# Routing by one key per expert in two layers, the last layer's shared down-weights in the idle half of the residual, and another order of the queue's transfers

## The chip, the core and the metric

One Trainium2 chip, one of its cores. The kernel is one program with five instruction streams: TensorE (PE in the profile; PEld is its weight loading), VectorE (DVE), ScalarE (ACT), GpSimd (POOL) and SyncE (SP), which here issues all direct transfers. The metric is the device time of one execution in microseconds (us).

## The reference, cut to what matters

The model has two layers over 256 context tokens and 256 image tokens, 1024 features wide, all in fp32. Each layer is a mixer of three branches followed by a mixture of experts. The change lies in the experts' part and at its edges:

```python
def moe_ffn(xf, w_router, router_bias, w_e_gate, w_e_up, w_e_down, w_s_gate, w_s_up, w_s_down):
    scores = jax.nn.sigmoid((xf @ w_router).astype(jnp.float32))
    biased = scores + router_bias
    group_score = lax.top_k(biased.reshape(N, N_GROUPS, N_EXPERTS // N_GROUPS), 2)[0].sum(-1)
    _, gidx = lax.top_k(group_score, TOPK_GROUPS)                 # 4 of 8 groups
    ...
    _, eidx = lax.top_k(masked, TOP_K)                            # 8 of 64 experts
    wts = jnp.take_along_axis(scores, eidx, axis=1)
    wts = wts / (wts.sum(-1, keepdims=True) + 1e-20) * ROUTED_SCALE
    routed = routed_experts(xf, eidx, wts, w_e_gate, w_e_up, w_e_down)
    return routed + swiglu(xf, w_s_gate, w_s_up, w_s_down)        # a shared expert for all tokens
```

An expert is `(silu(x @ w_gate) * (x @ w_up)) @ w_down` with a hidden width of 256. Its gate and up weights are 2 MB and its down weights 1 MB, so one layer's 64 experts are some 200 MB. Layer 0 sends all 512 tokens through its experts, layer 1 (the last) only the 256 image tokens; nothing reads the context half of the residual once layer 1's mixer is past.

## The kernel before, in words

**Stages.** Each layer runs the mixer (`mla`, `ml`, `rw`), the merge of the branches (`mg_*`), a norm (`norm_*`), the routing (`ro_*`), and the experts: `px_*` in layer 0, `ex_*` in layer 1. Each stage has a function per engine, and each engine runs its own in program order. Semaphores order the engines: `pe.wait_ge(ro["sel"], ...)` lets PE wait until the selection is made. Every line with `ch.link(...)` waits for its own result, so DVE's chain in the routing is serial.

**Routing.** PE makes the router's product (L1429) and turns the tokens round (L1438) for a row-wise copy in HBM (`hidden_rows`, stored by SP at L1728 or L2152). DVE (`ro_dve`) selects 8 experts a token; `r_sel` is the 0/1 result (L1567). PE sums it into each token's position at its expert (L1445) and the expert's count (L1448, L1450). Two small products spread the expert ranks (L1454, L1456), and `place_rows` (L1496 on) turns each position into a row number `r_at`. The rows are cut in units of 128, each holding the tokens of one to four experts. Then, for each tile of 128 tokens and each of its 8 choices, 32 times in layer 0 and 16 in layer 1: DVE picks the k-th chosen row out of `r_at` (L1591), builds two one-hot blocks `r_hot` and `r_val` (L1601, L1603), and PE multiplies them (L1463) into the list of which token stands in which row. From it come the indices of the gathers (L1614, L1616; semaphore `ro["dk"]`).

**The shared expert.** PE computes its gate and up products in two halves (`shared_gate_up`, L1720), one between the rank product and the one-hot products, the other behind them. Its weights lie in the tile `branches` (`GU_W[3]`). ACT and DVE make the hidden values from them (`sh["sig"]`, `sh["hid"]`). In layer 1 the shared down product (L2281) runs ahead of the first unit, from the buffer `DN5[0]` in which expert 0's down weights stand afterwards.

**Experts.** For each unit PE turns the gathered rows (L1860; L2286 and L2301 in layer 1), multiplies them by the gate and up weights (L1870; L2296), turns the hidden values and multiplies by the down weights (L1885; L2310). Layer 0 stores each row in HBM and adds them up per token later (L1958, L2121). Layer 1 scales each row by its weight while copying it out of the bank (ACT L2418, DVE L2486) and adds it to its token at once (L2316). These row weights `SW` come by a long way: DVE makes the choice weights, SP stores them in HBM (L2180, `choice_weight_rows`), and POOL gathers one column for each unit (L2222).

**The weights' queue.** SP issues every weight load, in the order of `px_sync` and `ex_sync`. The slots are four (five in layer 1), and a load into a slot waits until PE has finished with what stood there. Layer 0's experts are ranked by load, so its first loads wait for the ranks (`ro["end"]`); in layer 1 experts 0 to 3 are fixed in their slots, so their loads wait only for the end of the merge.

## Time and profile before

| | us |
|---|---|
| median of 3 runs (2644.52 to 2645.91) | 2645.62 |
| the profiled execution | 2642.83 |
| its span | 2640.6 |
| layer 0: product of the one-hot blocks begins, ends | 863.7, 881.5 |
| layer 0: first unit's gate product begins | 905.24 |
| layer 1: first unit's gate product begins | 2123.20 |
| layer 1: last unit's last product ends | 2621.99 |

The profiled execution took 2.2 us more than the span of its instructions. The page has the busy time of each engine (PE 2402.9 us, 91%; DVE 785.4; ACT 570.4; POOL 146.3) and the same in 40 slices of 66 us. A digit is the busy share in tenths, PEclk is the granted clock of TensorE, and the DMA rows are the share of the 16 transfer engines and what they moved. A busy PE isn't PE at its peak.

### The profile page before, as it was taken

How to read it: one execution, taken by the hardware profiler on the slowest of the kernel's cores; microseconds unless marked ns; L12 is line 12 of the kernel's file. 1: busy time of each engine (PE TensorE's matmuls, PEld its weight loads, DVE VectorE, ACT ScalarE, POOL GpSimd, SP SyncE). 2: the span in 40 equal slices, each digit the busy share in tenths (PEclk: the TensorE clock that was granted, in tenths of full speed). 3: DMA queues.
4: the chain of work that ended last, by engine and by line, in shares of the span. 5: the costliest groups of instructions: out<-in, count | busy, mean ns of one | idle time of the engine just before them, and what ended most of it. 6: DMA issues, size and time to landing. Idle time of an engine off the chain costs nothing.

```text
span 2640.6 us, 41238 instructions
## 1 busy us (share of the span) xinstructions
PE 2402.9 (91%) x17286; PEld 1365.7 (52%) x17286; DVE 785.4 (30%) x1929; ACT 570.4 (22%) x1132; POOL 146.3 (6%) x154
## 2 busy tenths in 40 slices
PE   7999988999998898999998799988999799967997
PEld 3466477644445443333333556767788644433444
DVE  1364455311114431111111525555411521111112
ACT  3455223300002011111111144433210111100111
POOL 0000000000000111111111000000000011100100
PEclk9999999999997799999999899999999699988999
DMA  7101142411102699999999631122331599999993
GB/s 321 71 10 41 37 157 103 188 64 64 64 0 110 243 422 420 413 406 424 403 408 393 260 146 67 70 70 94 143 147 64 204 393 423 419 408 417 413 423 163
DMA packets 67640, 599.72 MB, mean 227 GB/s; under 512 B 13182, under 2 KB 13310, under 8 KB 25600
## 3 DMA queue, kind: packets, MB, share of 16 engines
q1 hardware_dynamic: 50032, 555.09, 51.9%
q0 software_dynamic: 17424, 41.99, 4.2%
q8 instruction: 137, 2.24, 0.3%
q14 instruction: 47, 0.39, 0.0%
HBM read 588.63 MB, written 26.75 MB: 233 GB/s over the span
## 4 chain that ended last, share of the span: by engine, by line
PE 82%; DMA 7%; DVE 5%; issue 3%; ACT 2%; another core or an unknown queue 0%; SPq 0%; ACTq 0%; DVEq 0%
PE bank L1870 10%; PE bank L1345 9%; PE bank L2296 7%; PE bank L292 6%; PE bank L1885 5%; PE bank L2310 3%; PE bank L1360 3%; PE bank L1350 3%; PE bank L2316 3%; PE bank L384 3%; DMA ring<-in_wexp 2%; DMA arena<-in_wexp 2%; PE bank L1034 2%; PE bank L1049 2%; PE bank L309 1%
## 5 line engine op out<-in xcount | busy, mean ns | idle before, releaser
L1870 PE MATMUL bank<-ring,arena 128*32 128x512 f32 (+2 forms) x1248 | 297.5, 610 | 16.5 <-issue 15.2
L1345 PE MATMUL bank<-normed,ring 128*128 128x512 f32 (+1 forms) x768 | 255.5, 486 | 0.0
L2296 PE MATMUL bank<-ring,arena 128*32 128x512 f32 (+2 forms) x832 | 193.4, 621 | 18.1 <-issue 16.6
L1345 PEld LDWEIGHTS bank<-normed,ring 128*128 128x128 f32 x768 | 145.9, 190 | 101.8 <-issue 91.8
L1870 PEld LDWEIGHTS bank<-ring,arena 128*32 128x32 f32 (+2 forms) x1248 | 94.7, 131 | 154.0 <-issue 152.0
L292 PE MATMUL bank<-normed,ring 128*128 128x512 f32 (+1 forms) x416 | 160.5, 544 | 0.0
L1870 PE MATMUL bank<-branches,arena 128*32 128x512 f32 (+2 forms) x400 | 134.3, 594 | 6.3 <-issue 6.3
L1885 PE MATMUL bank<-arena 128*32 128x512 f32 (+2 forms) x384 | 112.8, 596 | 7.0 <-DMA arena<-in_wexp 3.3
L292 PEld LDWEIGHTS bank<-normed,ring 128*128 128x128 f32 x416 | 78.4, 190 | 77.8 <-issue 75.3
L2060 DVE TENSOR_TENSOR arena<-bank,arena 128x256 f32<-128x256 f32 x43 | 18.3, 425 | 324.0 <-ACT arena L1979 324.0
L2296 PE MATMUL bank<-normed,arena 128*32 128x512 f32 (+1 forms) x256 | 92.9, 644 | 21.0 <-issue 18.1
L2296 PEld LDWEIGHTS bank<-ring,arena 128*32 128x32 f32 (+2 forms) x832 | 55.9, 123 | 102.4 <-issue 102.4
L1799 POOL DMA_INDIRECT arena<-hidden_rows,block_slots x42 | 42.7, 1016 | 1167.5 <-DVE block_slots L1616 883.9
L1885 PE MATMUL bank<-ring,arena 128*32 128x512 f32 (+2 forms) x440 | 102.0, 596 | 4.0 <-issue 2.0
L2480 DVE TENSOR_TENSOR arena<-bank,arena 128x256 f32<-128x256 f32 x27 | 11.5, 425 | 301.2 <-ACT arena L2412 301.2
L2316 PE MATMUL bank<-arena 128*128 128x256 f32 x432 | 97.7, 380 | 1.2 <-DVE arena L2486 1.2
L2310 PE MATMUL bank<-arena 128*32 128x512 f32 (+1 forms) x400 | 82.1, 630 | 17.4 <-issue 16.8
L2296 PE MATMUL bank<-branches,arena 128*32 128x512 f32 (+1 forms) x208 | 94.7, 609 | 0.0
L1350 PE MATMUL bank<-branches,ring 128*128 128x512 f32 (+1 forms) x256 | 90.4, 486 | 0.0
L2316 PEld LDWEIGHTS bank<-arena 128*128 128x128 f32 x432 | 80.0, 190 | 12.6 <-issue 2.8
L1360 PE MATMUL bank<-arena,ring 128*128 128x512 f32 (+1 forms) x256 | 83.1, 486 | 2.6 <-DVE arena L1389 2.6
L1372 ACT ACTIVATE arena<-bank 128x512 f32<-128x512 f32 (+1 forms) x48 | 23.4, 490 | 286.2 <-PE bank L1345 286.2
(484 smaller groups left out, 3828.5 us busy)
## 6 DMA issues: line engine op xcount, KB each, us to landing
ring<-in_wexp SPq DMA_DIRECT2D x87, 2048.0 KB, 14.5
ring<-in_wst SPq DMA_DIRECT2D x54, 2048.0 KB, 8.4
arena<-in_wexp SPq DMA_DIRECT2D x70, 1024.0 KB, 20.4
branches<-in_wexp SPq DMA_DIRECT2D x31, 2048.0 KB, 13.8
ring<-in_wexp SPq DMA_DIRECT2D x60, 1024.0 KB, 12.1
normed<-in_wexp SPq DMA_DIRECT2D x12, 2048.0 KB
arena<-expert_rows SPq DMA_DIRECT2D x6, 2048.0 KB, 11.0
branches<-expert_rows SPq DMA_DIRECT2D x2, 2048.0 KB, 14.4
```

The lines of the kernel that those rows point to most:

```text
L292: last = nc.tensor.matmul(bank[:, c0:], weights[:, k, j0:j0 + n], H[:, k, c0:], start=(k == 0), stop=(k == KD - 1))
L384: last = nc.tensor.matmul(ps[j][:, c0:], w[:, k, (j % 4) * P:(j % 4 + 1) * P], H[:, k, c0:], start=(k == 0), stop=(k == KD - 1))
L1034: last = nc.tensor.matmul(ps[4 + pr][h, cc], NL[pr][h, cc], XT[pr][h, cc] if v else ident[h, h], start=True, stop=True)
L1049: last = nc.tensor.matmul(ps[pr][h, cc], ZT[pr][h, cc], X[pr][h, cc], start=True, stop=True)
L1345: last = nc.tensor.matmul(ps[2 * (n % 4)][:, c0:], wg[:, k, i * P:(i + 1) * P], H[:, k, c0:], start=(k == 0), stop=(k == KD - 1))
L1350: last = nc.tensor.matmul(ps[2 * (n % 4) + 1][:, c0:], wb[:, k, :], BR[:, k, c0:], start=(k == b0), stop=(k == b1 - 1))
L1360: last = nc.tensor.matmul(ps[m % 4][:, c0:], w[:, k, (m % 4) * P:(m % 4 + 1) * P], YM[:, k, c0:], start=(k == 0), stop=(k == KD - 1))
L1870: last = nc.tensor.matmul(ps[2 + s][r0:r1, :], XT_[:, s, k * P + r0:k * P + r1], wt[:, k, :], start=(k == 0), stop=(k == KD - 1))
L1885: last = nc.tensor.matmul(ps[5 + h][r0:r1, :], HDT[:, s, k * P + r0:k * P + r1], wt[:, k, h * 512:(h + 1) * 512], start=(k == 0), stop=(k ...
L2296: last = nc.tensor.matmul(ps[5][r0:r1, :], XT_[:, s, k * P + r0:k * P + r1], w[:, k, :], start=(k == 0), stop=(k == KD - 1))
L2310: last = nc.tensor.matmul(ps[6 + h][r0:r1, :], HDT[:, s, k * P + r0:k * P + r1], w[:, k, h * 512:(h + 1) * 512], start=(k == 0), stop=(k = ...
L2316: last = nc.tensor.matmul(acc(m), YB[s][:, m * P:(m + 1) * P], OH[s], start=False, stop=False)
```

## The change

1. **Routing, both layers.** The running count over the selected experts (`r_cs`) goes, and its place is taken by `r_keyed = r_at * r_sel`: a row number where an expert is chosen and zero elsewhere. One `max` a tile gives the 8 largest, which replaces the 8 picks a tile. The one-hot blocks are built for a whole tile, two broadcast operations for 8 choices, in two buffers; ACT multiplies each choice's part of `r_val` by its number. The positions are read from the bank, and are computed in pieces between the rank products, the last one behind them.
2. **Shared gate and up.** They are cut in four. One quarter stands ahead of the wait for the selection, two behind the last positions, and one behind the one-hot products. Their weights are issued before the stores of `hidden_rows`.
3. **Layer 0.** PE waits for the shared hidden values behind the first unit's gate product instead of ahead of its rows; DVE makes the second half behind its first copy.
4. **Layer 1.** The shared down weights go to `R[:, :, 0:TC]`, the context half of the residual, and expert 0's down weights go straight to their slot. The load of the fifth expert waits for the first gathered rows and stands ahead of the fourth's down weights. The store of the choice weights stands behind the first two loads of the list.
5. **Between the layers** the next layer's small weights and first two chunks are issued before the wait for the residual.
6. **Norms.** A `Ln` over one column runs ahead of the wait for the sum.

```diff
         def norm_act_rs(act, ch, l, w, c0):
+            ch.link(nc.scalar.activation(arena(4640, 1), cn("eps", 1), ACT.Ln))
             act.wait_ge(norm["mm"], nth(w, l) * NORM["mm"] + 1)
...
+            shared_gate_up(pe, l, 0, 0)
             pe.wait_ge(ro["sel"], l * RO["sel"] + 1)
-            for t in range(t0, TT):
-                for u in range(t0, t + 1):
-                    nc.tensor.matmul(ps[2][:, t * E:(t + 1) * E], ...)
...
+            for t in range(t0, TT - 2):
+                positions(t)
             pe.wait_ge(ro["rk"], l * RO["rk"] + 1)
             nc.tensor.matmul(ps[1][:, E:2 * E], ...).then_inc(ro["ranked"], 1)
+            positions(TT - 2)
             pe.wait_ge(ro["rk"], l * RO["rk"] + 2)
             nc.tensor.matmul(ps[1][:, 2 * E:7 * E], ...).then_inc(ro["ranked"], 1)
-            shared_gate_up(pe, l, 0)
+            positions(TT - 1).then_inc(ro["pos"], 1)
+            shared_gate_up(pe, l, 0, 1)
+            shared_gate_up(pe, l, 1, 0)
...
+            for n, t in enumerate(range(t0, TT)):
+                act.wait_ge(ro["hot"], l * RO["hot"] + n + 1)
+                for k in range(HOT):
+                    part = r_val[:, n % 2, k, 0:PLAN[l].n]
+                    nc.scalar.activation(part, part, ACT.Copy, scale=cn("choice", 1, n * TOPK + k)).then_inc(ro["hc"], 1)
...
-            for i, (t, k) in enumerate(chosen):
-                ch.add(V.scalar_tensor_tensor(r_junk[:, i % 2, :], r_cs[:, t, :], float(k + 1), r_at[:, t, :], ALU.is_equal, ALU.mult,
-                                              accum_out=r_dk[:, t, k:k + 1]))
-                ch.settle()
+            ch.link(V.tensor_tensor(r_keyed[:, t0:, :], r_at[:, t0:, :], r_sel[:, t0:, :], ALU.mult))
+            for t in range(t0, TT):
+                ch.add(V.max(r_dk[:, t, :], r_keyed[:, t, :]))
...
+            for n, t in enumerate(range(t0, TT)):
+                if n >= 2:
+                    dve.wait_ge(ro["hotm"], l * RO["hotm"] + (n - 1) * HOT)
+                ch.link(V.tensor_tensor(r_hot[:, n % 2, :, :], bcast(cn("count", P), 1, HOT), bcast(r_p[:, t, :], 2, P), ALU.is_equal))
+                V.tensor_tensor(r_val[:, n % 2, :, 0:at.n], bcast(cn("count", at.n), 1, HOT), bcast(r_u[:, t, :], 2, at.n), ALU.is_equal).then_inc(ro["hot"], 1)
...
         def px_pe(pe, l, before):
-            pe.wait_ge(sh["hid"], l * SHN["hid"] + 4)
...
                 if u:
                     rows_down(u - 1)
+                else:
+                    pe.wait_ge(sh["hid"], l * SHN["hid"] + 4)
...
         def ex_sync(sp, before):
+            sp.dma_start(R[:, :, 0:TC], wexp[l, E, :, GU_N:].rearrange("p (k n) -> p k n", k=KD)).then_inc(shared_down_in[0], 16)
+            down(0, 0, dn5_in[0][0])
...
             gate_up(3, 3, gu5_in[3][0])
+            sp.wait_ge(*rows_arrived(0))
+            fifth = sp.value_load(EJI[0:1, 4:5], min_val=0, max_val=E)
+            gate_up(fifth, 4, gu5_in[4][0])
             sp.wait_ge(sh["hid"], l * SHN["hid"] + 4)
             down(3, 3, dn5_in[3][0])
-            sp.wait_ge(cb["c"], weights_made)
-            sp.dma_start(wrow..., WK[:, TT - NX:, :]).then_inc(weights_kept[0], 16)
+            first_later = min(i for i, (last_use, _, _) in enumerate(at.loads) if last_use)
+            for i, (last_use, kind, p) in enumerate(at.loads):
+                if i == first_later:
+                    sp.wait_ge(cb["c"], weights_made)
+                    sp.dma_start(wrow..., WK[:, TT - NX:, :]).then_inc(weights_kept[0], 16)
...
         def _(sp):
-                if l:
-                    sp.wait_ge(sh["res"], l * SHN["res"])
                 for n, (m, j) in enumerate(ORDER_OF_USE[l]):
+                    if l and n == 2:
+                        sp.wait_ge(sh["res"], l * SHN["res"])
```

How this stands on the engines. First PE in layer 0, from the turning of the tokens to the first unit; `normed,branches` is the shared gate and up product, `bank<-arena` with 76 columns is the product of the one-hot blocks. Before:

```order
L1438 MATMUL bank<-consts,normed 128x128 x32
L1445 MATMUL bank<-arena,consts 128x64 x10
L1448 MATMUL bank<-arena,consts 128x64 x4
L1450 MATMUL bank<-consts,arena 64x64 x4
L1454 MATMUL bank<-arena,consts 128x64
L1456 MATMUL bank<-arena,consts 128x320
L1720 MATMUL bank<-normed,branches 128x512 x16
L1463 MATMUL bank<-arena 128x76 x32
L1467 MATMUL bank<-arena,consts 128x64
L1720 MATMUL bank<-normed,branches 128x512 x16
```

PE in layer 0 at the same place, now:

```order
L1439 MATMUL bank<-consts,normed 128x128 x32
L1728 MATMUL bank<-normed,branches 128x512 x8
L1446 MATMUL bank<-arena,consts 128x64 x4
L1448 MATMUL bank<-consts,arena 64x64 x4
L1453 MATMUL bank<-arena,consts 128x64 x3
L1460 MATMUL bank<-arena,consts 128x64
L1453 MATMUL bank<-arena,consts 128x64 x3
L1463 MATMUL bank<-arena,consts 128x320
L1453 MATMUL bank<-arena,consts 128x64 x4
L1728 MATMUL bank<-normed,branches 128x512 x16
L1473 MATMUL bank<-arena 128x76 x32
L1728 MATMUL bank<-normed,branches 128x512 x8
```

Eight shared products have moved ahead of the counts, eight stay behind the one-hot products where sixteen stood, and the ten position products are spread over three places. (A product counts once here; the trace shows two instructions for each.)

Then SP in layer 1, around the store of the choice weights; `TENSOR_LOAD` and `ISA` are the reading of an expert's number and the waits of a load. Before:

```order
L2155 DMA normed<-in_wexp 128x4096
L2158 ISA
L2158 DMA arena<-in_wexp 128x2048
L2180 DMA choice_weight_rows<-choice_weights 128x2x8
L2183 TENSOR_LOAD block_experts
L2183 ISA x2
L2155 ISA
L2155 DMA ring<-in_wexp 128x4096
```

SP in layer 1 at the same place, now, from the fourth expert's down weights on:

```order
L2168 DMA arena<-in_wexp 128x2048
L2168 ISA
L2168 DMA arena<-in_wexp 128x2048
L2198 TENSOR_LOAD block_experts
L2198 ISA x2
L2165 ISA
L2165 DMA ring<-in_wexp 128x4096
L2198 TENSOR_LOAD block_experts
L2198 ISA x2
L2165 ISA
L2165 DMA ring<-in_wexp 128x4096
L2197 DMA choice_weight_rows<-choice_weights 128x2x8
```

Two loads of 2 MB, which wait for the first unit's gate product, now stand ahead of the store.

## Rows read from the trace of the kernel before

**Rows 1.** The page's slices of 66 us: share of the transfer engines, in tenths
```profile
DMA  7101142411102699999999631122331599999993
```
**Rows 2.** Windows: length, busy PE, PEld, DVE, ACT, POOL; clock, DMA share, GB/s
```profile
870.00:875.00 5.00, 5.00 (x20) 4.56 (x20) 4.67 (x19) 0.00 (x0) 0.00 (x0) 0.50 0.64 269
905.00:1460.00 555.00, 518.32 (x2894) 199.52 (x2894) 100.48 (x241) 83.22 (x171) 82.74 (x84) 0.98 0.98 403
2115.00:2603.00 488.00, 424.80 (x2610) 198.95 (x2608) 69.39 (x169) 53.94 (x105) 53.80 (x55) 0.94 0.99 411
```
**Rows 3.** Chain of waits through layer 0's routing: start, us, what
```profile
833.33 4.53 PE bank L1445 x20
...
840.65 0.22 DVE arena L1580
...
853.56 0.24 DVE arena L1591 x2
...
862.11 0.19 DVE arena L1594
...
865.89 15.59 PE bank L1463 x56
...
884.83 16.32 PE bank L1720 x32
...
905.24 7.76 PE bank L1870 x32
```
**Rows 4.** Timeline of both routings: start, us, engine, line, what, [idle before]
```profile
830.52 1.08 ACT L1481 ACTIVATE arena<-bank 128x512 f32<-128x512 f32 x2 [0.67 <-DMA hidden_rows<-arena]
831.31 0.61 DVE L1562 MAX8 arena<-arena 128x8 f32<-128x64 f32 x4
...
2067.40 1.08 ACT L1481 ACTIVATE arena<-bank 128x512 f32<-128x512 f32 x2 [0.19 <-PE bank L1438]
```
**Rows 5.** Operations like the new ones, lines by form: busy, mean ns
```profile
L1225 DVE TENSOR_TENSOR arena<-arena 128x1024 f32<-128x1024 f32 x1 | 1.2, 1218 | 0.0
L2032 ACT ACTIVATE arena<-consts,choice_weights 128x128 f32<-128x128 f32 x8 | 2.4, 390 | 0.0
```
**Rows 6.** Chain of waits, layer 1's routing and first units
```profile
2073.41 0.63 PE bank L1450 x4
...
2091.17 8.84 PE bank L1463 x32
...
2103.27 9.53 PE bank L1720 x32
...
2114.18 7.17 PE bank L2281 x32
2121.36 0.45 PE bank L2286 x4
...
2123.20 7.02 PE bank L2296 x32
...
2143.32 4.08 another core or an unknown queue
```
**Rows 7.** Timeline of SP (issue only) and POOL in layer 1
```profile
2112.82 0.33 SPq L2155 DMA_DIRECT2D branches<-in_wexp  x1
...
2129.90 0.38 SPq L2180 DMA_DIRECT2D choice_weight_rows<-choice_weights  x1
2131.04 9.60 SPq L2155 DMA_DIRECT2D ring<-in_wexp  x3
...
2136.03 1.00 POOL L2222 DMA_INDIRECT arena<-choice_weight_rows,block_slots  x1 [29.73 <-DMA choice_weight_rows<-choice_weights]
```
**Rows 8.** Chain of waits, later in layer 1: one load of 2 MB
```profile
2305.93 29.53 DMA ring<-in_wexp
```
**Rows 9.** Chain of waits between the layers, and at the last norm
```profile
1520.73 8.52 DMA ring<-in_wst
...
2626.51 1.28 ACT L267
```
**Rows 10.** Timeline of ACT between the layers
```profile
1526.97 7.97 ACT L286 ACTIVATE normed<-normed,modv,mod_scale 128x256 f32<-128x256 f32 x16 [0.76 <-DVE normed L273]
```

106 lines of the change are left out of this document (49 added, 57 removed).

## The prediction

> **What bounds the kernel.** I read the page first. Its slices [rows 1] show the transfer engines full in two stretches, 924 to 1452 us and 2112 to 2600 us. They are the two layers' experts, some 200 MB of weights each. The windows put numbers on it [rows 2]: in layer 0's expert stage the transfers are busy for 0.98 of the time, at 403 GB/s, and PE for 518 of 555 us; in layer 1's it is 0.99 and 411 GB/s, with PE busy for 425 of 488 us. So layer 0's stage is bound by both at once and layer 1's by the transfers. Neither gets shorter inside; what helps is that it starts earlier, or that the weights' stream has fewer holes at its start.
>
> The next view is the chain of waits through layer 0's routing [rows 3]. From the selection at 833 us to the first unit's product at 905.24 us, 72 us pass, in which transfers and PE do little for the experts. The chain alternates between DVE's serial steps, the product of the one-hot blocks, and the second half of the shared gate and up product. Layer 1's chain [rows 6] has the same steps, shorter, and two that layer 0 lacks: the shared down product (7.17 us) and, at 2143.32, a wait of 4.08 us of ACT for the gathered row weights.
>
> **Layer 0, step by step.**
> 1. A quarter of the shared product goes ahead of the counts. It can begin when ACT's last copy is done, 830.52 + 1.08 = 831.6 [rows 4]. It is 16 instructions. At full speed 32 of 256 columns take 7.17 us [rows 6], so 16 of 512 take 7.2; PE has idled before and starts at half clock, which I put at 1.4 us. It ends at 840.2. The counts took 840.65 - 837.86 = 2.8 us [rows 3] and take 1.4 to 2.8 now: DVE gets them 0.9 to 2.4 us later. I take 1.7.
> 2. The last position products, 8 instructions of 4.53 / 20 = 0.23 us [rows 3], stand behind the rank product, where DVE has 0.9 us of other work. Another 0.9 late; but a copy of 0.4 is gone. Together 2.2 us late.
> 3. The 32 picks take 862.11 - 853.56 = 8.55 us [rows 3]. In their place come one product over 256 elements (0.45) and four maxima, 0.61 [rows 4]. DVE gains 7.5 us here, and begins with the one-hot blocks at 857.7 instead of 863.0.
> 4. A tile's blocks are 1024 and 8 x 76 = 608 elements. The trace has no operation with such broadcast operands. The nearest row is 1024 elements without them, 1.22 us [rows 5]; so 1.2 + 0.8 = 2.0 us a tile. The bounds are that and twice as much. Two tiles are ready by 861.7.
> 5. PE isn't ready then. Behind the positions it has half of the shared product, which took 15.3 us there before and ends at 864.9 now. PE becomes what is late; this hides step 3 in part, and would hide step 4 up to 3.6 us a tile.
> 6. The one-hot product is 64 instructions. Before, it ran from 863.7 to 881.5 at the pace of DVE, and the granted clock fell to 0.50, which is 1.2 GHz [rows 2]. At PE's own pace an instruction takes 0.22 us at that clock (step 2) and 0.11 at 2.4 GHz, by the turning of rows, 0.45 for 4 [rows 6]. That bounds the phase at 8 and 14.5 us. I take 11.6, since it starts at full clock and such short products let it fall before. It ends at 876.5, 5.0 us earlier.
> 7. ACT multiplies 32 parts of 76 columns. Eight of 128 columns with a factor from memory take 2.4 us [rows 5], 0.3 each, less than PE's 0.22 x 2 for a choice. Hidden behind PE; if PE runs at full clock it costs up to 2 us.
> 8. Behind the one-hot product 16 instructions stand instead of 32: 7.2 us less of the 16.32 [rows 3]. Then the wait for the hidden values goes (they are needed 9 us later): of the 4.1 us from 901.15 to 905.24 some 1.4 remain, one turning and one copy. Together 9.9 us.
>
> Sum: 5.0 + 9.9 = 14.9 us earlier at the first unit, between 11 and 18 by the bounds. From there on nothing in layer 0's stage changes and transfers and PE are both full, so the whole stage moves by it.
>
> A rule of the Trainium skill speaks against step 7. ScalarE: Activation LUTs, What ACT_TABLE_LOAD costs, gives an activation 186 ns and 0.833 ns a column, 93 ns more for a factor from memory, and 93 less in a row of them. For 76 columns that is an estimate of 0.25 us each, 8.0 us in 32. By that rule the sum stays as long as PE needs more, and would lose some 2 us if it needed 0.22 a choice; the row of 0.3 us for 128 columns agrees with it.
>
> **Layer 1.** The same steps, in the same order. The quarter of the product runs from 2068.5 [rows 4] for 3.6 us, at a clock that the turning of the tokens before it keeps up, the counts are done 0.9 us earlier than 2074.04 [rows 6]. The picks give 3.6 us. PE is through with its 32 instructions of the shared product, 9.5 us long as those of L1720 [rows 6], at about 2089; the one-hot product takes 32 x 0.11 to 0.22 instead of 8.84 us and ends at 2094.6, 5.4 us earlier than 2100.0. Sixteen fewer instructions behind it give 3.6. The shared down product waits for the hidden values as before and takes its 7.17 us as before: the gathered rows are there before it is done, so it fills no wait. The first rows are turned 9.0 us earlier, at 2112.4, and the first gate product ends at 2121.2 instead of 2130.2.
>
> Here the queue's new order takes it back. The store of the choice weights was issued at 2129.90 and POOL went on at 2136.03 [rows 7]. Now it is issued behind two loads that wait for the first gate product: these go out at 2122.1 and 2123.2, and the store at 2123.7. Loads stand behind one another in this queue: one issued at 2305.93 landed 29.5 us later [rows 8], while 2 MB into an empty one took 8.5 [rows 9]. So the store waits for 4.2 MB, at 411 GB/s 10.2 us, and POOL goes on at 2135 to 2137, no earlier than before. ACT, ready at 2134.3, waits about 13 us instead of 4.1, and PE goes on at 2147.4 as before. What remains is the weights' stream: it starts 9.0 us earlier and has one load of 1 MB (2.5 us) less to do, but runs dry before the first two loads (3.7 us) and again while PE stands (5.3 us). That is 2.5 us, of which I take 1.5.
>
> DMA: Bandwidth & Descriptors, Queues, rings and completion order, of the Trainium skill states that each transfer engine takes its descriptors in the order of the ring and alternates between rings by packets. By this the store on SP's ring pays for both loads and the sum stands, while POOL's gathers, on a ring of their own, pay for a packet at a time.
>
> **The rest.** Between the layers the wait of 8.52 us for the first chunk goes [rows 9]. But PE's product there needs the normed tiles, which ACT makes one in 1.0 us from 1526.97 to 1534.94 [rows 10]; PE began at 1529.3 and ended one product behind ACT. It ends there again: nothing, at most 1 us. In the norms the table load stands ahead of the wait already. The new `Ln` over one column is hidden in four norms and stands behind the load of 1.28 us in the last [rows 9]: 0.2 us lost. The load in 1024 pieces of 1 KB into the residual has over 40 us; I cost it at nothing, and should it take three times as long, still nothing.
>
> **Sum.** 2642.83 - 14.9 - 1.5 + 0.2 = 2626.6 for the profiled execution. The median of the runs shown is 2.8 us above it, so 2629.
>
> **The rivals.**
> - *The store isn't late.* If it lands in some 6 us whatever stands before it, the row weights come by 2141 and the 9.0 us of layer 1 carry through, less the first hole, with the load saved: 8 instead of 1.5. 2623 us. For it: only 6.1 us [rows 7], behind several MB. Against it: the load of 29.5 us [rows 8].
> - *The blocks bind.* Broadcast operands at twice the time (4 us a tile), or ACT's parts in series with PE, lengthen the one-hot product to its old length. Only the fillers' gain of step 8 remains in layer 0: 9.9. 2634 us.
> - *The start is worth less.* Layer 0's stage keeps its end because the stream is what counts and its loads come no earlier. Then 1.5 and little more: 2642 us. Against it: the stream's first load behind the initial ones waits for the first gate product.
> - *Slower: the row weights.* PE in layer 1 stands until ACT has the first of them. Each further 2 MB ahead of the store or of POOL's gathers costs 5.1 us. From 2152 us on for POOL's first gather, 16 us later than before, layer 0's gain is eaten; with the gathers also late, 2650. Against it: just two loads stand ahead.
> - *The change doesn't do what it says*, PE's fillers standing on the path instead of in waits: 2644.
>
> **How the numbers follow.** Forecast 0.62, store not late 0.12, blocks bind 0.12, start worth less 0.07, slower 0.04, no effect 0.03. The forecast's own terms give 2625 to 2634; with the first two rivals the range is 2619 to 2637. Within 0.2%, which is 5.3 us, a measurement of this kernel can't tell a change from none. Faster 0.93, same 0.03, slower 0.04.
>
> **What would show it.** Right: the first gate product of layer 0 at about 890 and of layer 1 at about 2099 (2114 less 15); the one-hot product back to back on PE; ACT's wait for the row weights near 13 us; layer 0's expert stage unchanged at 555 us. Wrong: DVE or ACT ahead of every one-hot instruction in the waits; POOL's first gather of weights less than 14 us after the first gate product; an expert stage of layer 0 that has grown by what its start has won.

## The result, and the profile after

The changed kernel takes 2616.33 us (median of 4 runs, 2613.38 to 2616.77) against 2645.76 of the kernel before (now 4 runs, 2644.52 to 2652.57): a ratio of 0.9881, 95% interval 0.9863 to 0.9899. The forecast was 2629, range 2619 to 2637: the sign was right, but the time lies below the range, and the gain is 29 us where some 17 were forecast. The profiled executions differ by 26.55 us (2642.83 and 2616.28) where the sum had 16.2. Measured from landmarks that both kernels have (the norm's product, L262, the last thing ahead of the router; and the first gate product), this is where it arose:

| stretch (profiled executions, us) | before | after | forecast | measured |
|---|---|---|---|---|
| start to layer 0's norm product | 798.36 | 801.21 | 0 | +2.85 |
| from there to layer 0's first gate product | 106.88 | 87.55 | -14.9 | -19.33 |
| from there to layer 1's norm product | 1145.71 | 1145.55 | 0 | -0.16 |
| from there to layer 1's first gate product | 72.25 | 58.53 | -9.0 | -13.72 |
| from there to the end of the span | 517.40 | 521.26 | +7.7 | +3.86 |

The first line is unchanged code, at a mean granted clock of 0.98 in both profiles; over all profiles below it lies between 792 and 806. So differences of a few us are read from such stretches, not from spans.

The chain of waits of the changed kernel through layer 0's routing, to be held against [rows 3] (start, us, what):

```profile
834.67 8.65 PE bank L1728 x16
843.32 0.84 PE bank L1446 x8
844.16 0.62 PE bank L1448 x8
...
851.82 15.36 PE bank L1728 x32
867.18 1.76 PE bank L1473 x16
868.93 0.02 issue
868.96 1.24 DVE arena L1612
870.20 0.02 issue
870.22 0.80 DVE arena L1613
...
871.45 4.19 PE bank L1473 x32
...
878.72 8.77 PE bank L1728 x16
```

The picks (L1591) are gone from it; PE's own shared product (L1728) leads up to the one-hot product, which takes 8.5 us instead of 17.8. The windows over it, to be held against [rows 2] (length, busy PE, PEld, DVE, ACT, POOL; clock, DMA share, GB/s):

```profile
865.00:870.00 5.00, 5.00 (x34) 3.80 (x32) 1.04 (x1) 1.73 (x7) 0.00 (x0) 1.00 1.00 426
870.00:875.00 5.00, 4.25 (x36) 4.11 (x34) 2.90 (x4) 3.96 (x16) 0.00 (x0) 1.00 0.99 421
888.00:1445.00 557.00, 522.18 (x2899) 200.84 (x2898) 104.40 (x244) 85.33 (x177) 82.75 (x84) 0.98 0.98 404
2093.00:2576.00 483.00, 419.38 (x2574) 191.42 (x2572) 70.93 (x170) 53.22 (x104) 54.12 (x56) 0.93 0.98 406
```

The granted clock over the one-hot product is 1.00 (2.4 GHz) where it was 0.50. Layer 0's expert stage keeps its length and its rate (403 and 404 GB/s). Layer 1's is a little less full (406 GB/s instead of 411), and by the table above it lasts 3.9 us longer. In the page, the transfers' slices show the same two full stretches as [rows 1], each beginning earlier:

```profile
DMA  7101032511101899999999811122341699999993
```

Layer 1, the chain of waits, against [rows 6]:

```profile
2060.04 1.06 PE bank L1453 x4
...
2070.14 3.98 PE bank L1473 x32
...
2077.30 5.13 PE bank L1728 x16
...
2083.86 7.14 PE bank L2370 x32
2091.00 0.45 PE bank L2295 x4
...
2092.84 7.04 PE bank L2305 x32
...
2101.55 13.64 DMA choice_weight_rows<-choice_weights
2115.24 0.48 issue
2115.76 0.19 issue
2115.95 5.99 DMA arena<-choice_weight_rows,block_slots
2122.02 0.70 ACT arena L2437
```

The store of the choice weights does what the forecast said: issued behind two loads of 2 MB, it lets POOL go on after 14.4 us, and ACT waits 11.03 us for the row weights. PE stands for 8.5 us:

```profile
2115.00:2120.00 5.00, 0.00 (x0) 0.00 (x0) 0.00 (x0) 0.00 (x0) 3.14 (x4) 0.78 1.00 419
```

### The profile page after: what moved, and what is told of

Same layout as the page of the kernel before. It is cut to its first block, busy times and chain, and to the rows that moved or that the text cites. A ratio compares the mean times of both kernels' runs of the same rounds, so it can differ in the third digit from the quotient of the medians.

```text
span 2614.1 us, 41116 instructions
## 1 busy us (share of the span) xinstructions
PE 2390.2 (91%) x17286; PEld 1348.4 (52%) x17286; DVE 763.1 (29%) x1747; ACT 582.9 (22%) x1185; POOL 146.1 (6%) x154
## 4 chain that ended last, share of the span: by engine, by line
PE 82%; DMA 8%; DVE 4%; issue 3%; ACT 2%; SPq 0%; ACTq 0%; DVEq 0%; POOLq 0%
PE bank L1878 11%; PE bank L1346 9%; PE bank L2305 6%; PE bank L293 6%; PE bank L1893 5%; PE bank L2319 3%; PE bank L1361 3%; PE bank L1351 3%; DMA arena<-in_wexp 3%; PE bank L2325 3%; PE bank L385 3%; DMA ring<-in_wexp 2%; PE bank L1035 2%; PE bank L1050 2%; PE bank L310 1%
## 5 line engine op out<-in xcount | busy, mean ns | idle before, releaser
L1878 PE MATMUL bank<-ring,arena 128*32 128x512 f32 (+2 forms) x1248 | 298.3, 613 | 17.9 <-issue 16.2
L2305 PEld LDWEIGHTS bank<-ring,arena 128*32 128x32 f32 (+2 forms) x832 | 55.4, 124 | 102.9 <-issue 102.8
L1989 ACT ACTIVATE arena<-bank 128x256 f32<-128x256 f32 x43 | 16.5, 384 | 316.7 <-PE bank L1878 316.7
## 6 DMA issues: line engine op xcount, KB each, us to landing
ring<-in_wexp SPq DMA_DIRECT2D x87, 2048.0 KB, 14.4
ring<-in_wexp SPq DMA_DIRECT2D x59, 1024.0 KB, 10.3
branches<-expert_rows SPq DMA_DIRECT2D x2, 2048.0 KB, 13.8
```

Of the source, the lines that this page charges most:

```text
L1878: last = nc.tensor.matmul(ps[2 + s][r0:r1, :], XT_[:, s, k * P + r0:k * P + r1], wt[:, k, :], start=(k == 0), stop=(k == KD - 1))
L2305: last = nc.tensor.matmul(ps[5][r0:r1, :], XT_[:, s, k * P + r0:k * P + r1], w[:, k, :], start=(k == 0), stop=(k == KD - 1))
```

## The experiments

Sixteen kernels ran, two of them repeats; each is the changed kernel with one edit unless said otherwise. The table has all of them; in the text a single letter stands for the kernel whose name begins with it. Columns: the median; the ratio to the kernel before, timed beside it, with its interval; then, from the profile, us from layer 0's norm product to its first gate product (A), layer 0's expert stage from there to the shared down product (B), the same as A in layer 1 (C), and from layer 1's first gate product to the end of the span (D). The landmarks are read from PE's timeline, which puts them 0.1 us off the chain's.

| kernel | median | ratio | A | B | C | D |
|---|---|---|---|---|---|---|
| before | 2645.76 | 1 | 107.0 | 557.0 | 72.3 | 517.5 |
| changed | 2616.33 | 0.9881 (0.9863 to 0.9899) | 87.7 | 555.8 | 58.6 | 521.3 |
| s_changed_again | 2614.67 | 0.9883 (0.9865 to 0.9901) | 86.3 | 559.0 | 58.6 | 521.1 |
| f_picks_added | 2632.63 | 0.9954 (0.9935 to 0.9974) | 95.8 | 556.9 | 67.5 | 519.2 |
| n_picks_covered | 2619.55 | 0.9894 (0.9871 to 0.9917) | 89.1 | 556.7 | 60.5 | 519.4 |
| p_blocks_single | 2627.33 | 0.9925 (0.9903 to 0.9946) | 94.2 | 556.4 | 65.9 | 518.8 |
| q_picks_alone | 2636.58 | 0.9955 (0.9938 to 0.9973) | 102.1 | 556.8 | 68.8 | 518.6 |
| b_fillers_back | 2623.35 | 0.9916 (0.9888 to 0.9944) | 90.2 | 556.9 | 64.1 | 519.0 |
| c_hidden_wait | 2612.38 | 0.9882 (0.9852 to 0.9912) | 88.6 | 557.3 | 58.6 | 518.2 |
| a_store_first | 2618.04 | 0.9888 (0.9864 to 0.9912) | 86.3 | 556.0 | 61.4 | 519.1 |
| k_early_weights | 2610.85 | 0.9871 (0.9848 to 0.9895) | 86.3 | 556.5 | 58.4 | 518.2 |
| e_no_shared_down | 2611.22 | 0.9862 (0.9836 to 0.9888) | 87.8 | 556.1 | 53.3 | 523.6 |
| h_old_slot | 2615.10 | 0.9879 (0.9850 to 0.9908) | 87.9 | 556.0 | 58.5 | 521.3 |
| d_edges_back | 2616.04 | 0.9875 (0.9856 to 0.9894) | 87.9 | 559.8 | 58.5 | 521.4 |
| j_quarter_swap | 2612.40 | 0.9873 (0.9856 to 0.9890) | 81.9 | 560.1 | 55.4 | 521.4 |
| m_best | 2609.96 | 0.9855 (0.9838 to 0.9872) | 83.3 | 559.9 | 54.2 | 518.5 |
| m_again | 2606.43 | 0.9846 (0.9831 to 0.9862) | 81.8 | 559.9 | 54.5 | 518.3 |
| u_without_memsets | 2610.95 | 0.9861 (0.9843 to 0.9879) | 81.9 | 557.6 | 53.9 | 518.4 |

### Why the one-hot product became so short

```diff
+            for i in range((TT - t0) * TOPK):      # f_picks_added: behind the max of each tile
+                ch.add(V.scalar_tensor_tensor(r_junk[:, i % 2, :], r_keyed[:, t0, :], 1.0, r_at[:, t0, :], ALU.is_equal, ALU.mult, accum_out=...))
+                ch.settle()
+            shared_gate_up(pe, l, 1, 1)            # n_picks_covered: this too, ahead of the one-hot product
...
-            shared_gate_up(pe, l, 1, 1)            # and not behind it
```

> The changed kernel with 32 serial picks in layer 0 and 16 in layer 1 added ahead of the one-hot blocks on DVE (their results are not used), 8.5 and 4.3 us, so that DVE is as late there as before. PE then stands some 2 us in layer 0 and 5 us in layer 1 between its fillers and the one-hot product. Theory A (the product runs at PE's own pace and full clock, 0.13 us an instruction, whatever a pause of 2 us does): layer 0's first gate product comes 2 to 3 us later, layer 1's 4.3 later, 6 to 7 us in all. Theory B (the pause, or the pace of DVE, lets the clock fall to 1.2 GHz, as in the prediction's half): the one-hot product takes 12 to 15 us in layer 0, and the first gate product comes 7 to 10 us later, 11 to 15 us in all. If the picks were worth all their time, 12.8 us.

> The kernel with the added picks once more (32 and 16 serial operations of DVE whose results are not used), and in it PE's last quarter of the shared gate and up product moved ahead of the one-hot product, so that PE comes to it later than DVE and without a pause. Theory (PE's pause of 3.8 us ahead of the one-hot product let the clock fall; what DVE does meanwhile is nothing to it): the 64 instructions take 8 to 8.6 us in layer 0 instead of 12.8 with the pause, and the 32 in layer 1 take 4.0 instead of 7.1. Layer 0's first gate product: the picks are hidden, but the gathers start only behind them; 90 to 95 us from the start of the norm's product (87.7 in the changed kernel, 95.8 with the picks alone). Rival (the late picks themselves, or the pace of ACT's parts, slow the product): 12 us again in layer 0 and 7 in layer 1.

PE's timeline in layer 0, with the picks added (start, us, what, [idle before it and what ended that]):

```profile
848.17 16.23 PE L1732 MATMUL bank<-normed,branches 128*128 128x512 f32 x32
868.17 12.75 PE L1473 MATMUL bank<-arena 128*128 128x76 f32 x64 [3.76 <-ACT arena L1497]
```

and with the picks added and covered:

```profile
850.92 22.64 PE L1732 MATMUL bank<-normed,branches 128*128 128x512 f32 x48
873.39 3.69 PE L1474 MATMUL bank<-arena 128*128 128x76 f32 x32
877.83 4.17 PE L1474 MATMUL bank<-arena 128*128 128x76 f32 x32 [0.75 <-ACT arena L1497]
884.66 0.43 PE L1478 MATMUL bank<-arena,consts 64*128 64x64 f32 x2 [2.66 <-DVE arena L1633]
889.14 1.97 PE L1872 MATMUL bank<-consts,arena 128*128 128x128 f32 x8 [4.05 <-DMA arena<-hidden_rows,block_slots]
```

The windows over the one-hot product, first without cover, then with it:

```profile
870.00:875.00 5.00, 5.00 (x26) 5.00 (x25) 2.88 (x3) 3.95 (x16) 0.00 (x0) 0.50 0.73 308
875.00:880.00 5.00, 5.00 (x25) 5.00 (x25) 1.15 (x2) 2.58 (x9) 0.00 (x0) 0.50 0.01 3
```

```profile
875.00:880.00 5.00, 4.25 (x37) 4.11 (x36) 3.94 (x4) 2.58 (x11) 0.00 (x0) 1.00 1.03 437
```

Both kernels have the same picks and the same blocks. They differ in whether PE stands 3.76 us ahead of the product. With the pause the clock is at 0.50 in the product and its 64 instructions take 12.75 us; without it the clock stays at 1.00 and they take 8.6 from first to last. Theory B of the first run had the mechanism and the size in layer 0 (A of the table 8.1 to 9.5 us later, forecast 7 to 10), but not the sum: with C 8.9 us later it is 17 to 18 us, and 16 to 18 by the medians, where it said 11 to 15. The theory of the second held in layer 0's product; A is 89.1 where it said 90 to 95, and layer 1's product took 4.8 us instead of 4.0, behind a wait of 1.6 us that the cover left there. In layer 0 the covered kernel still waits 4.05 us for the gathered rows.

```diff
-                ch.link(V.tensor_tensor(r_hot[:, n % 2, :, :], ...))      # p_blocks_single
-                V.tensor_tensor(r_val[:, n % 2, :, 0:at.n], ...)
+                for k in range(TOPK):
+                    ch.link(V.tensor_scalar(r_hot[:, n % 2, k, :], cn("count", P), r_p[:, t, k:k + 1], None, ALU.is_equal))
+                    V.tensor_scalar(r_val[:, n % 2, k, 0:at.n], cn("count", at.n), r_u[:, t, k:k + 1], None, ALU.is_equal)
```

> The changed kernel with the one-hot blocks built one choice at a time, 16 operations a tile instead of two, all else (picks by max, ACT's multiplication, PE's order) as changed. Theory: a tile takes DVE 4.4 us as before instead of 2.0; two tiles are ready when PE comes from its fillers, the third and fourth are not; PE stands for them some 5 us in layer 0 and hardly in layer 1 (both tiles ready at about 2076 instead of 2070, so up to 5 us there too), and the clock falls in part of it. 5 to 9 us later in layer 0 and 4 to 7 in layer 1, 9 to 16 in all. Rival (PE's fillers cover it): less than 3 us in all.

A is 6.5 to 7.9 us later and C 7.3, 14 to 15 together; the median is 11 to 13 us above the changed kernel's. The theory held, with layer 1's part just above its range (4 to 7). PE waits 2.36 us for the third tile, and the product goes on at half clock:

```profile
866.36 4.05 PE L1473 MATMUL bank<-arena 128*128 128x76 f32 x32
872.76 3.70 PE L1473 MATMUL bank<-arena 128*128 128x76 f32 x16 [2.36 <-ACT arena L1497]
876.69 3.69 PE L1473 MATMUL bank<-arena 128*128 128x76 f32 x16 [0.23 <-ACT arena L1497]
```

```diff
-            for i, (t, k) in enumerate(chosen):                           # q_picks_alone, on the kernel before
-                ch.add(V.scalar_tensor_tensor(r_junk[:, i % 2, :], r_cs[:, t, :], float(k + 1), r_at[:, t, :], ...))
+            ch.link(V.tensor_tensor(r_cs[:, t0:, :], r_at[:, t0:, :], r_sel[:, t0:, :], ALU.mult))
+            for t in range(t0, TT):
+                ch.add(V.max(r_dk[:, t, :], r_cs[:, t, :]))
```

> The kernel before with one part of the change alone: the picks by one product and one max a tile (and the choice weights by the row number, in the same number of operations). DVE is 7.5 us earlier ahead of the blocks in layer 0 and 3.6 in layer 1, as the prediction had it. Theory (the parts need one another): PE's half of the shared product then ends behind DVE, and only PE's waits ahead of the one-hot product go, 2.4 us in layer 0 and 2.2 us in layer 1; the blocks are still built one by one, so the product keeps the pace of DVE. 4 to 5 us faster than before, about 2641. Rival (each part is worth its own time wherever it stands): 11 us, 2634.

In this kernel `r_dk` moves to a place that layer 1 clears before its choice weights are made, so their values in layer 1 are not the reference's; no instruction is more or less for it. The ratio is 0.9955, that is 7 to 16 us by its interval; A and C together are 8.4 us shorter. So the theory's 4 to 5 was too little, and the rival's 11 us lies in the interval. The waits ahead of the product go as expected, but the product gets shorter too (14.4 us instead of 17.8 in layer 0, 7.7 instead of 8.8 in layer 1), since it begins at full clock. The clock then falls, without a pause of PE, at the pace of the blocks:

```profile
863.00:868.00 5.00, 4.68 (x31) 3.72 (x29) 3.53 (x14) 0.60 (x1) 0.00 (x0) 1.00 1.00 424
868.00:873.00 5.00, 4.65 (x19) 3.81 (x18) 4.67 (x19) 0.00 (x0) 0.00 (x0) 0.65 0.98 418
873.00:878.00 5.00, 5.00 (x20) 4.55 (x19) 4.23 (x17) 0.00 (x0) 0.00 (x0) 0.50 0.38 161
```

The product's first instructions run back to back. From 866 us on two come in every 0.55 us, which is DVE's time for the blocks of a choice, with 0.11 us of idle between the pairs, and the clock falls in that stretch. PE's busy time (4.68, 4.65, 5.00 of 5.00 us) doesn't show it; the number of its instructions does.

### What the cut of the shared product is worth

```diff
-            shared_gate_up(pe, l, 0, 0)                 # b_fillers_back: not ahead of the counts
             pe.wait_ge(ro["sel"], l * RO["sel"] + 1)
...
+            shared_gate_up(pe, l, 0, 0)                 # behind the positions
             shared_gate_up(pe, l, 0, 1)
-            shared_gate_up(pe, l, 1, 0)
...
+            shared_gate_up(pe, l, 1, 0)                 # behind the one-hot product
             shared_gate_up(pe, l, 1, 1)
```

> The changed kernel with the shared gate and up product in two halves again: half of it behind the positions and half behind the one-hot product, none ahead of the counts. Theory: the 16 instructions behind the one-hot product come back on the path, 8.8 us in layer 0 and 5.1 us in layer 1; the counts come up to 5.6 us earlier in layer 0, which PE's fillers then hide from 0 to 5 us; so layer 0's first gate product is 4 to 9 us later and layer 1's 3 to 5 later, 7 to 14 us in all, most likely 10. Rival (the quarter ahead of the counts delays DVE's chain by as much as it saves): layer 0 less than 2 us later, the whole 3 to 5 us. Second rival (without the quarter the clock is low during the counts and at the start of the fillers): 2 us more than the theory.

A is 2.5 to 3.9 us later and C 5.5; the median is 7 to 9 us above, at the lower end of the theory's 7 to 14. In layer 0 the rival (less than 2 us) was nearer. PE's timeline shows why:

```profile
833.35 1.97 PE L1445 MATMUL bank<-arena,consts 128*128 128x64 f32 x8 [3.79 <-DVE arena L1583]
835.25 1.12 PE L1447 MATMUL bank<-consts,arena 128*64 128x64 f32 x8
...
843.49 14.92 PE L1728 MATMUL bank<-normed,branches 128*128 128x512 f32 x32
858.25 3.69 PE L1472 MATMUL bank<-arena 128*128 128x76 f32 x32
...
870.13 16.98 PE L1728 MATMUL bank<-normed,branches 128*128 128x512 f32 x32
```

Sixteen more instructions stand behind the product, and take 8.2 us more, but everything ahead of them is 5.6 us earlier against the norm's product (870.13 - 798.16 and 878.72 - 801.21 us, less the 0.1 between the two views). PE is busy from the counts on. The quarter can begin only when ACT's last copy is made, 33.6 us behind the norm's product, and the counts could begin at 35.2 without it: it fills 1.6 of the 3.8 us of wait. Behind it the counts run at full clock, 1.6 us instead of 3.0. The rest of the quarter is paid in either place.

```diff
+            pe.wait_ge(sh["hid"], l * SHN["hid"] + 4)   # c_hidden_wait: ahead of the first rows
...
-                else:
-                    pe.wait_ge(sh["hid"], l * SHN["hid"] + 4)
```

> The changed kernel with layer 0's wait for the shared hidden values ahead of the first rows again, and DVE making their second half ahead of its first copy. Theory: PE stands 2 to 3 us between its last quarter and the turning of the first rows, for ACT's sigmoid and two DVE products; layer 0's first gate product comes 2.7 us later (2.0 to 3.2), the rest of the kernel is the same: + 2.7 us. Rival (the gathered rows are late anyway): less than 0.5 us.

PE waits 2.14 us ahead of the first rows, where it had not waited; A is 0.9 to 2.3 us later, less than the theory's 2.7. The median can't show it (2612.4, below the changed kernel's).

### Layer 1's row weights

```diff
+            sp.wait_ge(cb["c"], weights_made)           # a_store_first: ahead of the list
+            sp.dma_start(wrow..., WK[:, TT - NX:, :]).then_inc(weights_kept[0], 16)
             for last_use, kind, p in at.loads:
...
+            for part in range(3):                       # k_early_weights: this too
+                choice_weights(ch, l, part)
             rows_in(0)
-            for part in range(3):
-                choice_weights(ch, l, part)
```

> Layer 1's store of the choice weights stands ahead of the list of loads again; nothing else differs from the changed kernel. Theory (the store pays for the two loads ahead of it): POOL's first gather of row weights comes some 6 us behind the store instead of 14.4 us, so at about 2106 to 2108 instead of 2115.95; ACT's wait of 11.0 us before its first scaled copy shrinks to 1 to 5 us, and PE resumes 5 to 8 us earlier. At the end 4 to 6 us are left, about 2611. Rival (the weights' stream sets layer 1's end, as the prediction had it): PE resumes earlier, but the end moves by less than 1.5 us, 2615 to 2616. Second rival (the store pays for what is in flight anyway): POOL's gather comes no earlier and nothing moves.

> As the kernel with the store first, and DVE makes layer 1's choice weights ahead of its first copy of gathered rows, in the 8.85 us in which it waits for PE, instead of behind it. Theory: the choice weights (6.5 us of DVE) are ready at about 2091 instead of 2100, the store lands by 2097, the row weights are there by 2104, and ACT never waits for them; PE's pause between unit 1's hidden values and its down product is about 7 us or less (12.8 in the changed kernel). Against the changed kernel 6 to 8 us earlier at that point and 5 to 8 at the end, about 2610. Rival (the stream sets the end): less than 1.5 us, 2615 to 2616. Second rival: DVE's copy of rows comes late, up to 0.5 us lost at the first gate product.

SP's, POOL's and ACT's timelines, with the store first:

```profile
2100.14 0.38 SPq L2194 DMA_DIRECT2D choice_weight_rows<-choice_weights  x1
```

```profile
2102.45 1.00 POOL L2235 DMA_INDIRECT arena<-choice_weight_rows,block_slots  x1 [23.92 <-DMA choice_weight_rows<-choice_weights]
```

```profile
2111.89 0.69 ACT L2435 ACTIVATE arena<-bank,arena 128x512 f32<-128x512 f32 x1 [1.28 <-PE bank L2317]
```

and SP's and POOL's with the weights made early:

```profile
2088.77 0.38 SPq L2194 DMA_DIRECT2D choice_weight_rows<-choice_weights  x1
```

```profile
2099.60 1.00 POOL L2235 DMA_INDIRECT arena<-choice_weight_rows,block_slots  x1 [21.45 <-DMA choice_weight_rows<-choice_weights]
```

ACT's wait of 11 us is gone in both. From layer 1's first gate product to ACT's first scaled copy it is 29.2 us in the changed kernel and 19.5 in these two, as in the kernel before (2142.63 - 2123.20 = 19.4). At the end it is worth much less. The stretch D is 521.1 to 521.4 in the changed kernel and those that differ from it little, 518.2 to 519.1 here; but some kernels with the late store (b, c, p, f, n) have 518.2 to 519.4 too. The medians are 2618.0 and 2610.9 against 2616.3 and 2614.7.

So the first theory, 4 to 6 us at the end, failed: alone the early store shows nothing there. Its profile has a part of the reason in code that the edit doesn't touch: the shared products of layer 1 took 9.7 and 6.6 us instead of 8.3 and 5.2, and C is 61.4. With the weights made early the median is 4 to 5 us lower (theory 5 to 8, rival under 1.5), which the intervals don't separate from nothing. The closest pair is j and u below, which differ in these two edits alone and were timed side by side: D is 521.4 and 518.4, the medians are 2612.4 and 2611.0. Of 9.7 us some 3 arrive in the stretch D; what of it reaches the whole is not shown.

```diff
-                for m in range(KD):                     # e_no_shared_down
-                    for k in range(2):
-                        nc.tensor.matmul(acc(m), R[:, 4 * k + m // 2, ...], SH[...], start=..., stop=False)
+                for m in range(0, KD, 2):
+                    nc.tensor.matmul(acc(m), R[:, m // 2, 0:P], SH[:, TC:T], start=True, stop=False)
```

> The changed kernel with layer 1's shared down product cut to the four instructions that open the banks (the shared expert's part is missing from the output). Theory (the prediction's: the gathered rows are there before the product is done, and it stands on the path): the first gate product of layer 1 comes 6 to 7 us earlier, since 7.1 us of product go; the stage behind it is bound by the transfers, so 4 to 7 us remain at the end. Rival (the product fills the wait for the rows): the rows then are what PE waits for, and the first gate product moves by less than 2 us.

C is 5.3 us shorter, which is what the 24 instructions took (7.14 - 1.97 us), so the product stands on the path and fills no wait for rows: the theory, with the four remaining ones dearer than it said. D is 2.3 us longer, and ACT waits 13.86 us for the row weights. C and D together are 3 us shorter and the median 3 to 5, where the theory left 4 to 7.

```diff
-            sp.dma_start(R[:, :, 0:TC], wexp[l, E, :, GU_N:]...).then_inc(shared_down_in[0], 16)   # h_old_slot
-            down(0, 0, dn5_in[0][0])
+            sp.dma_start(DN5[0], wexp[l, E, :, GU_N:]).then_inc(shared_down_in[0], 16)
...
+            sp.wait_ge(sh["gu"], SHN["gu"] * L + 1)
+            down(0, 0, dn5_in[0][0])
```

> The changed kernel with layer 1's shared down weights in the first down slot again; expert 0's down weights (1 MB) are loaded there behind the shared down product, ahead of the fifth expert's. Theory: the load is issued some 8 us later and needed by PE at the first unit's down product, some 20 us behind; it adds no wait, the transfers carry the same bytes, and the first stretch of the stream, which runs dry around there, hides it: 0 to 1 us later. Rival (the early load of expert 0 is worth its 2.5 us of the stream, which is full from there on): 2 to 3 us later at the end, with the first gate product unmoved.

All four stretches are those of the changed kernel within 0.2 us. The new place of the shared down weights is worth nothing here.

```diff
-            ch.link(nc.scalar.activation(arena(4640, 1), cn("eps", 1), ACT.Ln))   # d_edges_back
...
-                    if l and n == 2:
+                    if l and n == 0:
                         sp.wait_ge(sh["res"], l * SHN["res"])
```

> The changed kernel with two small edits undone: the wait for the residual stands ahead of the next layer's first two chunks again, and the Ln over one column that runs ahead of the norm's sum goes. Theory (the prediction's): between the layers PE ends behind ACT's normed tiles in any case, nothing to 1 us later; at the last norm 0.2 us earlier; the whole is within 1 us of the changed kernel. Rival (PE began there late before and paid for it): from the last product of layer 0's combination to the end of the merge's first block 1.6 to 3 us later.

The median is 2616.04. From the shared down product to the merge's first product it is 67.1 us here and 64.9 to 66.1 in the changed kernel's two profiles. PE waits there 5.83 us for the chunk (5.75 in the kernel before); in the changed kernel it waits 4.73 us for ACT's first normed tile and then five times more for the next ones, 1.35 us in all. So it begins earlier and ends behind ACT all the same: the theory.

### Is there more to gain, and where does the stream cap it

```diff
+            shared_gate_up(pe, l, 1, 1)                 # j_quarter_swap; DVE reads ps[3] behind shared_hidden(0)
             pe.wait_ge(ro["rk"], l * RO["rk"] + 3)
             nc.tensor.matmul(ps[3][:, 7 * E:8 * E], ones[0:E, :], r_cnt[0:E, :], ...)
-            shared_gate_up(pe, l, 1, 1)
...
-            for s in range(2):                          # m_best: this, j and k; u_without_memsets: j and k alone
-                ch.add(V.memset(XG[s], 0.0))            # behind the one-hot blocks
```

The repeat of the changed kernel and m_again have no edit of their own.

> Four edits on the changed kernel together: the two in which layer 1's choice weights are made and stored early; the two memsets of DVE that stand ahead of the rank chain go behind the one-hot blocks; and PE's last quarter of the shared gate and up product goes ahead of the small product of the expert numbers, for which PE waited 2.7 us (DVE reads that product behind the first half of the shared hidden values). Theory: layer 0's first gate product 2.5 us earlier than in the changed kernel, from the wait filled; layer 1's 2.5 us earlier from the same and 1 to 2 from the memsets, since there DVE's chain is what is late; and 3 us at the end from the weights as in the run before. 8 to 9.5 us together, a median of 2607 to 2609. Rival (the gathered rows become late: POOL's first gather starts 10 us ahead of their turning in layer 0): nothing of it in layer 0, 2610 to 2612.

> The changed kernel unaltered, as the common measure for the runs with small effects: those timed so far lie within 6 us of it, and unchanged stretches of the program differ by up to 5 us between executions. Expected: median 2614 to 2618; layer 0's expert stage (first gate product to the shared down product) 555 to 557 us if that is its length for a start at 88 us from the norm's product. If it shows 559 to 560 here too, the longer stage of the two kernels in which it was seen is chance.

> The changed kernel with one edit: PE's last quarter of the shared gate and up product stands ahead of the small product of the expert numbers, in both layers. Both first gate products come 2.6 to 4.4 us earlier. Theory A (layer 0's expert stage moves as a whole with its start, as it did for the change itself): it keeps 556 us, and the whole gains 4 to 6 us, 2610 to 2612. Theory B (the changed kernel's start has caught up with the weights' stream, whose first loads wait for the ranks and not for PE): the stage grows to 559 to 560 us and ends where it did; only layer 1's part is left, 0 to 3 us, 2614 to 2616.

> The four edits together once more, unaltered, beside the common measure on one chip. Theory B: layer 0's stage takes 559 to 560 us again, and the end of that stage stands 643 us behind the norm's product as in the changed kernel. Theory A: 556 us, the longer one was chance. The median against the changed kernel: 5 to 7 us less by A and B alike for the early choice weights and layer 1's start, up to 10 by A.

> The same without the edit of the memsets. Layer 1's counts then come some 2 us later than with it. Theory (PE's quarter ahead of the counts and its fillers behind them are what is late in layer 1 too): the one-hot product of layer 1 begins within 1 us of the kernel with all four, and the median is the same within 1.5 us. Rival (DVE's chain is what is late, as the chain of waits of the changed kernel shows it): 1 to 2 us later.

PE's timeline with the four edits (the repeat):

```profile
868.21 4.18 PE L1473 MATMUL bank<-arena 128*128 128x76 f32 x32 [0.75 <-ACT arena L1497]
872.23 7.08 PE L1725 MATMUL bank<-normed,branches 128*128 128x512 f32 x16
879.23 0.43 PE L1478 MATMUL bank<-arena,consts 64*128 64x64 f32 x2
```

The wait of 2.66 us is gone, and the quarter takes 7.08 us instead of 8.77, since the clock had fallen with that wait (it was 0.50 from 879 to 882 us in the changed kernel). A is 81.8 to 83.3 in the four kernels with the swap and 86.3 to 87.9 in the seven whose layer 0 is unaltered: 4.9 us on average. B is 557.6 to 560.1 and 555.8 to 559.8. From the norm's product to the end of layer 0's stage, A and B together, it is 643.3, 642.0, 641.8 and 639.5 with the swap; without it 643.5, 645.3, 642.4, 642.8, 643.8, 643.9 and 647.7. The means are 641.7 and 644.2: of 4.9 us about half arrives. At layer 1's norm product nothing of it is left: from layer 0's to there it is 1231.4 to 1236.8 us with the swap and 1231.1 to 1236.7 without, with means of 1233.1 and 1233.4, though the code between is the same. A stage of 559 came without the swap too (the repeat), so a single profile could not have told it. The median of j, 2612.4, lies between the two theories (2610 to 2612, and 2614 to 2616); neither holds alone.

The memsets are worth nothing in the profiles: from layer 1's norm product to its one-hot product it is 36.0 (changed, u) and 37.5 us (j) with them in place and 36.6 with them moved. PE's quarter ahead of the counts is late there anyway; the 0.91 us of each in the chain of waits was not a cost. The medians were to be the same within 1.5 us and are not (2611.0 for u, 2606.4 for the repeat of m and 2610.0 for its first run); no stretch of layer 1 in the profiles shows where such a difference would come from (C 53.9 and 54.2 to 54.5, D 518.4 and 518.3 to 518.5).

The version with all four has the lowest ratios: 0.9855 and 0.9846 against 0.9881 and 0.9883, medians 2610.0 and 2606.4 (forecast 2607 to 2609) against 2616.3 and 2614.7. Only the second is clear of the changed kernel timed beside it, and neither is clear of u.

## Why the forecast was right, and where it was wrong

The forecast was too high, outside its range. In the profiled executions 10.3 us more were gained than the sum had: 4.4 at layer 0's start, 4.7 at layer 1's start and 3.8 behind it, against 2.9 us lost in unchanged code ahead of both. Three steps failed. Step 6 put layer 0's one-hot product at 11.6 us, and it took 8.5. Layer 1's shared product ahead of the one-hot product was put at 9.5 us and took 8.3, from an earlier start. And "PE goes on at 2147.4 as before" took ACT's wait of 4.08 us for slack that was used up, where nearly 5 us were free: PE went on 8.2 us earlier, and the stretch behind layer 1's start got 3.9 us longer instead of 7.7.

- *Layer 0, steps 1 to 5* held. Counted from the norm's product, the quarter ended 0.3 us later than forecast, the fillers 0.6 earlier (867.18 for 864.9 + 2.85), and DVE began with the one-hot blocks at 860.56, as forecast (857.7 + 2.85). PE and not DVE is what is late there.
- *Step 6 failed, and it is the largest single miss in layer 0.* It priced the one-hot product between half and full clock, 11.6 us, "since it starts at full clock and such short products let it fall before". It took 8.5, with its bubble of 0.75, at full clock throughout. An instruction of this product took 0.13 us at full clock, a little more than the 0.11 of the turning of rows that step 6 took for its lower bound. What let the clock fall before was not the shortness of the products but the pause ahead of them and the pace of DVE between them; either is enough (a pause in f, against n, and in p; DVE's pace alone in q). The change removes both at once, and that is why the picks, worth 7.5 us of DVE to the forecast and hidden "in part" behind PE, cost 8 to 9 us in each layer when put back. The parts aren't a sum: undone one at a time, the picks, the blocks and the cut of the shared product cost 17 to 18, 14 to 15 and 8 to 9 us in A and C together, more than the 33 us that the change won there.
- *Steps 4 and 7* held: a tile's blocks took 1.24 + 0.80 us, the 2.0 of the forecast. ACT's parts took 4.09 / 16 = 0.26 us each, which agrees with the estimate from the Trainium skill, ScalarE: Activation LUTs, What ACT_TABLE_LOAD costs (0.25), and they stayed hidden behind PE but for the first of the third tile (0.4 us).
- *Step 8* had the right end (13.1 us behind the product, forecast 13.8) for partly wrong reasons. It credited the quarter moved from there with 7.2 us and charged its new place 1.7; undoing the cut costs only 2.5 to 3.9 in layer 0. The wait for the hidden values is 2.1 us long in c, where 2.7 were forecast.
- *Layer 1's start* was 13.7 us earlier instead of 9.0. The fillers ended 3.2 us earlier against the norm's product than forecast (they took 8.26 us instead of 9.5 and began 2 us sooner), the one-hot product another 0.6. A part of this is luck: in the profiles with this part of PE's program unaltered, the fillers took 8.2 to 8.7 us in eight and 9.5 to 9.9 in six (a, f, j, p and both of m). The mean granted clock over them was 0.86 in the changed kernel and 0.73 in a. That the shared down product fills no wait was right (e).
- *Layer 1's row weights: right wait, wrong consequence.* ACT's wait was forecast at 13 us and is 11.0, the way from the store to POOL at 11 to 13 and is 14.4; the store paid for the loads ahead of it, 14.4 us behind two of 2 MB and 2.3 with the store first (a). The Trainium skill, DMA: Bandwidth & Descriptors, Queues, rings and completion order, has each transfer engine take its descriptors in ring order; the traces agree. But the forecast took the row "2143.32 4.08 another core or an unknown queue" [rows 6] for ACT's wait for the row weights, and so all 11.4 us from POOL's gather to PE's next product for the gathers' time. The timeline of the kernel before has it otherwise:

```profile
2142.63 0.69 ACT L2418 ACTIVATE arena<-bank,arena 128x512 f32<-128x512 f32 x1 [1.28 <-DMA arena<-choice_weight_rows,block_slots]
2147.42 0.38 ACT L2415 ACTIVATE arena<-bank 128x256 f32<-128x256 f32 x1 [4.10 <-remote]
```

- The first scaled copy began at 2142.63 after 1.28 us of idle, the same 1.28 as with the weights long there (a). The 4.08 us belong to the instruction behind it, which copies hidden values and waits for nothing of the gathers. (With the weights early the same copy waits 1.82 us for PE. PE's turning that it waits for was done at 2145.10 in the kernel before; what held it for 2.3 us more stays open.) There were nearly 5 us of slack, those 4.1 and some 0.6 between the landing of the weights and ACT's first scaled copy (an estimate: the first gather took 5.99 us in the changed kernel), and the late store ate those first. So PE did not go on "as before" but 8.2 us earlier against the norm's product.
- *The stream in layer 1* was to take back 7.5 of 9 us; it took 3.9 of 13.7. The forecast counted the holes at the stage's start as lost, and credited 2.5 us for a load of 1 MB less; undoing that load's new place (h) changes nothing, so this term was nought. The windows show 0.98 of the time busy at 406 GB/s where it was 0.99 and 411, so the stage is a little less full. The limit shows in e, where D grows by 2.3 us of the 5.3 won ahead of it, and in k, where of 9.7 us some 3 arrive.
- *Layer 0's stage moves as a whole* held for these 19 us (557.0 us long, and 555.8 and 559.0 in the changed kernel's two profiles). For the next 5 us of the swap it held by half at best.
- *The rest* held: nothing between the layers that can be measured (-0.16 us in the table), and nothing lost by the shared down weights' load in pieces.

What stays open: how much the late store costs at the end (0 to 5 us by the medians), since D varies by 3 us among kernels that have the same store. No run takes apart the other order of the loads (the shared weights ahead of the stores of `hidden_rows`, the fifth expert's load ahead of the fourth's down weights) or the positions in pieces.

## What to carry to other kernels

Price a short product twice, at either clock, and ask what PE does just ahead of it and between its instructions: work on another engine that is hidden behind PE only after a pause, or only at that engine's pace, also costs the clock. A wait in a chain is somebody's wait: look up in the engine's own timeline which instruction it stands before, and what its neighbours wait in the ordinary case, before you make it the slack of a transfer. And moving filler from behind a serial chain to ahead of it gains only the idle time that it fills, and what a higher clock then saves in the work behind it.

## What the runs showed of the hardware

- The clock fell from 1.00 to 0.50 after a pause of 3.76 us (f) and again after one of 2.36 us in the midst of short products (p); it also fell where PE stood no longer than 0.11 us at a time, while its short instructions came at the pace of DVE, two in 0.55 us (q), although the profile counts PE as busy for 4.65 of 5.00 us. Back to back, the same instructions ran at 1.00 from first to last (the changed kernel, n).
- The same quarter of 16 instructions ahead of the counts took 8.65 to 8.80 us in some profiles and 7.10 in others, and the longer time came behind the shorter wait (2.2 to 2.4 us, and 2.7 to 2.9). It did so in one and the same kernel (the changed one and its repeat), and makes 1.4 us of A's spread.
- The small store took 2.3 us from issue to POOL's going on with nearly nothing left ahead of it (a, where the last load had been issued 15 us before), 10.8 us behind four loads issued 5 to 9 us before (k), and 14.4 us right behind two of 2 MB.
- Comparisons of DVE with broadcast operands run as those without: 1024 elements in 1.24 us, and 1.22 in [rows 5].
